# A two-block fp32 transformer kernel: output steps spread over the last attention heads, second weight slots waited for by pieces, one tile centred ahead of the roots, sixteen idle products, one gate copy released sooner

## The reference

```
block 1: mod = silu(c) @ ada_w + ada_b; h = rmsnorm(x)*(1+scale)+shift
         q,k,v,gates = h @ w_in; 8 sliding-window heads and 8 causal heads, d = 64
         x += gate1 * ((sig(ga)*(ya @ w_branch_a) + sig(gb)*(yb @ w_branch_b)) @ w_out)
         x += gate2 * (relu(h2 @ w_mlp_in)**2 @ w_mlp_out); x = rmsnorm(x)
block 2: short convolution mixer, layer_norm, SwiGLU (2816), layer_norm,
         forgetting attention (16 causal heads, logits + F[t] - F[s]) @ w_o, layer_norm,
         SwiGLU, layer_norm
```

## Time and profile before

| | us |
|---|---|
| median of 3 runs | 1969.68 (1968.35 to 1969.92) |
| the profiled execution, its own time | 1967.05 |
| its span, first to last instruction | 1965.3 |
| PE busy | 1906.1 (97%) |
| DVE busy | 1180.5 (60%) |
| ACT busy | 779.4 (40%) |
| POOL busy | 343.6 (17%) |
| mean granted TensorE clock | 0.992 |

### The profile page before, as it was taken

The page is one execution under the profiler, slowest core; times in us unless marked ns, Lnnn a source line. Parts: engine busy times, 40 slices in busy tenths (PEclk is TensorE's granted clock), DMA queues, the critical chain, the costliest instruction groups (busy, mean ns, idle before and its releaser), DMA issues.

```text
span 1965.3 us, 22312 instructions
## 1 busy us (share of the span) xinstructions
PE 1906.1 (97%) x8952; PEld 1577.2 (80%) x8952; DVE 1180.5 (60%) x1853; ACT 779.4 (40%) x1180; POOL 343.6 (17%) x307
## 2 busy tenths in 40 slices
PE   4999999999999999999999999999999999999997
PEld 3788888878888887888788888877898778888886
DVE  6687665576676745665655644476777754433446
ACT  4677622352223235222422222256677442222223
POOL 4323111021111112002300000036533130000003
PEclk9999999999999999999999999999999999999998
DMA  9522366266566434432545432313211223223221
GB/s 333 150 84 70 134 223 237 88 226 221 217 209 219 150 107 158 164 127 86 213 173 192 173 127 86 108 65 129 70 44 65 88 85 100 93 90 103 95 99 43
DMA packets 126232, 267.54 MB, mean 136 GB/s; under 512 B 4576, under 2 KB 33264, under 8 KB 126129
## 3 DMA queue, kind: packets, MB, share of 16 engines
q1 hardware_dynamic: 121168, 248.59, 37.0%
q0 software_dynamic: 4960, 17.53, 2.5%
HBM read 261.84 MB, written 8.45 MB: 138 GB/s over the span
## 4 chain that ended last, share of the span: by engine, by line
PE 70%; DVE 3%; ACT 2%; POOL 2%; issue 1%; DVEq 0%; POOLq 0%; ACTq 0%
PE ps L624 22%; PE ps L626 22%; PE ps L625 22%; PE ps L784 1%; PE ps L773 0%; ACT t L1212 0%; PE ps L762 0%; ACT t L1216 0%; POOL t L2316 0%; PE ps L801 0%; PE ps L802 0%; PE ps L800 0%; DVE t L1628 0%; DVE t L1613 0%; POOL t L2125 0%
## 5 line engine op out<-in xcount | busy, mean ns | idle before, releaser
L624 PE MATMUL ps<-t 128*128 128x512 f32 (+1 forms) x2504 | 966.7, 386 | 10.3 <-POOL t L2220 4.2
L626 PE MATMUL ps<-t 128*128 128x512 f32 (+1 forms) x2504 | 958.9, 383 | 0.0
L625 PE MATMUL ps<-t 128*128 128x512 f32 (+1 forms) x2504 | 955.0, 381 | 0.0
L1549 DVE TENSOR_TENSOR t<-t 128x2048 fp32r<-128x2048 f32 x133 | 305.4, 2296 | 440.4 <-ACT t L1163 440.2
L624 PEld LDWEIGHTS ps<-t 128*128 128x128 f32 x2504 | 470.7, 188 | 104.5 <-POOL t L2125 5.6
L626 PEld LDWEIGHTS ps<-t 128*128 128x128 f32 x2504 | 470.3, 188 | 96.4
L625 PEld LDWEIGHTS ps<-t 128*128 128x128 f32 x2504 | 470.5, 188 | 90.8 <-issue 1.0
L1163 ACT ACTIVATE t<-t 128x2048 fp32r<-128x2048 f32 x133 | 254.3, 1912 | 612.8 <-PE ps L626 605.3
L1613 DVE SCALAR_TENSOR_TENSOR t<-ps,t 128x512 f32<-128x512 f32 x184 | 131.7, 748 | 81.4 <-PE ps L626 78.0
L1561 DVE CUSTOM_DVE_ANT_0 t<-t 128x1024 f32<-128x1024 f32 x144 | 174.8, 1255 | 6.7 <-DMA t<-in_adakv_t 3.5
L2125 POOL TENSOR_TENSOR t<-t 128x512 fp32r<-128x512 f32 x88 | 115.5, 1332 | 196.8 <-ACT t L1170 196.2
(11 more groups left out here) (171 smaller groups left out, 1526.1 us busy)
## 6 DMA issues: line engine op xcount, KB each, us to landing
t<-in_ada SPq DMA_DIRECT2D x48, 1024.0 KB, 5.9
t<-in_gate SPq DMA_DIRECT2D x22, 1024.0 KB, 5.1
t<-in_up SPq DMA_DIRECT2D x22, 1024.0 KB, 5.1
t<-in_down SPq DMA_DIRECT2D x22, 1024.0 KB, 5.0
t<-in_w_in SPq DMA_DIRECT2D x17, 1024.0 KB, 5.7
t<-in_w_mlp_in SPq DMA_DIRECT2D x16, 1024.0 KB, 5.3
t<-in_w_mlp_out SPq DMA_DIRECT2D x16, 1024.0 KB, 5.0
t<-in_ada_t POOLq DMA_DIRECT2D x13, 1024.0 KB, 6.0
```

The source lines that it names most:

```text
L624: pe.matmul(o, wh, xh, start=first, stop=False)
L625: pe.matmul(o, wh, xl, start=False, stop=False)
L626: return pe.matmul(o, wl, xh, start=False, stop=last)
L1549: dve.tensor_tensor(WL[:, n % NW, :], raw[:, n % NRAW, :], WH[:, n % NW, :].bitcast(F), ALU.subtract).then_inc(w_lo_d.sem, w_lo_d.up("slot ...
```

## The change

It does five things. (1) The "o" job gets the units of kt 5 and 6, and the quotas of block 2 become 8 for heads 0 to 7, 7 for heads 8 to 11 and 2 for heads 12 to 15; after the last head only kt 7 is left of this slot. (2) `gemm_a` waits for the pieces of a pieced slot one by one, ahead of the tile that reads each. (3) In n4, n5 and n6 DVE centres one tile ahead of the wait for `rs`, and in the loop the next tile only. (4) Ahead of the third pair PE runs sixteen products of 256 columns. (5) ACT's copy of the gates waits for the first of the two writes of `AF`.

```diff
@@ job_units @@
             for kt in range(5):
                 yield ("unit", job, i, kt)
+        for kt in (5, 6):
+            for i in range(2):
+                yield ("unit", job, i, kt)
         return
-STEPS2 = attention_steps(["causal"] * 16, JOBS2, [8] * 12 + [3] * 4, AT_FOX + 3)
+STEPS2 = attention_steps(["causal"] * 16, JOBS2, [8] * 8 + [7] * 4 + [2] * 4, AT_FOX + 3)
@@ gemm_a @@
-                    slot_lo(on, n)
+                    pieced = n in PIECED
+                    if not pieced:
+                        slot_lo(on, n)
...
                         xh, xl, ready = src(kt)
+                        if pieced:
+                            on.wait_ge(w_lo_p, "slot", n, kt % 4)
@@ program_pe @@
-            for n, us in ((0, (0, 1)), (0, (2, 3)), (1, (0, 1, 2, 3)), (0, (4, 5)), (1, (4,)), (0, (6, 7)), (1, (5, 6, 7))):
+            for n, us in ((0, (0, 1)), (0, (2, 3)), (1, (0, 1, 2, 3)), (None, ()), (0, (4, 5)), (1, (4,)), (0, (6, 7)), (1, (5, 6, 7))):
+                if n is None:
+                    for _ in range(16):
+                        pe.matmul(psum[3][:, 0:256], ident, cst[:, 0:256], start=True, stop=True)
...
-                o_tile(AT_O, k, (5, 6, 7), 6 + k)
+                o_tile(AT_O, k, (7,), 6 + k)
@@ program_act @@
-            on.wait_ge(d_fox, "sum rows")
+            on.wait_ge(d_fox, "sum rows", 0)
@@ normed, program_dve @@
                 if layer:
-                    for k in range(3):
-                        centre(k)
+                    centre(0)
...
-                    if layer and k + 3 < KT:
-                        centre(k + 3)
+                    if layer and k + 1 < KT:
+                        centre(k + 1)
```

## The result

The changed kernel takes 1977.37 us (median of 4 runs, 1975.59 to 1978.97) beside 1969.01 for the kernel before (4 runs, 1966.61 to 1969.92): 8.36 us more, ratio 1.0041 with a 95% interval of 1.0028 to 1.0053. The forecast was 1972.7, in a range from 1968.5 to 1976.0. All medians are of executions in the fast state, which leaves out a single one of 7349 us, of the kernel before with one tile centred ahead.

What follows compares the result with a forecast made beforehand. PE, busy 97% of the span, was taken as the bound. Terms 6.9 - 0.75 - 0.55 - 0.2 - 0.6 - 1.8 + 0 = +3.0 took the profiled 1967.05 to 1970.05; plus 2.63 to the median: 1972.7 us, range 1968.5 to 1976.0.

Steps and rivals of the forecast that it cites:

- The products: Ahead of the third pair, sixteen idle products fill no wait and raise no clock, so cost their length: +6.9 us.
- the rival that hides them: At the third pair, the products cost nothing because a later PE wait takes the 6.9 back: 1965.8 us, chance 8%.
- Centring and pieces: One tile centred ahead gives n4 -0.75 us; pieces waited for singly give n4 -0.55, n3 -0.2, n6 -0.6.
- n5: Three centrings done by the roots' end, as in n6: 0.05 us at most, left out; no wait for pieces either.
- The units: Last heads: moved units fill 3.25 us of PE's idle time, a new wait ahead of kt 7 costs 1.45: -1.8.
- The first rival: Last heads: units lengthen the DVE and ACT chain and fill nothing, +1.45 for -1.8, time 1976.0 us, chance 14%.
- The gate copy: First gated head: ACT's copy comes sooner but isn't in the chain to PE's first score: 0, bound -0.3 us.
- The clock rival: Moved waits shift PE's half-clock stretches elsewhere, 1.8 to 3 us either way: 1970 or 1975.5 us, chance 12%.
- The sign: Whole kernel, beyond 0.2%: slower 0.30, faster 0.08, same 0.62.

Runs made afterwards that it cites:

- the fourth kernel: Changed kernel without the sixteen idle products and with three tiles centred ahead, keeping pieces, heads and gate copy: 1968.98 us beside 1970.25 before, ratio 0.9991.
- the kernel with three units: the fourth kernel plus three units of the next output slot ahead of the first kt 7: 1966.40 us beside 1969.39 before, ratio 0.9988.

## Why the prediction was wrong

**The products: right.** +6.9 was forecast from six records; the runs give 6.3 to 7.3, the timelines 6.7 to 6.9. They neither fill a wait nor hold a clock, and the rival that hides them is out.

**Centring and pieces: the step that failed.** They were to give -2.1 together (n4 -1.3, n3 -0.2, n6 -0.6) and gave +2.3 (n4 +0.64, n3 -0.05, n6 +1.73); that is 4.4 of the 5.4 us by which the sum was short (+8.36 for +3.0). The sentence is "The two added centrings take 0.3 to 0.6 of that". I had the time at which DVE ends tile 7's low half, 950.23, and the time at which PE wants it, and I moved only PE's. DVE was taken to have slack at the end because it has gaps there; they are used up by the two operations of 0.6 each, and then two more low halves fall behind POOL's operations. In the changed kernel the last low half is ready at 962.49. Moved back by the 10.8 that the kernel is late there, that is 951.7: 1.5 later than before, where at most 0.6 was allowed, while PE comes 1.9 sooner. And I looked at tile 7 alone; tiles 5 and 6 wait too, and with three tiles centred ahead the wait that is left (0.4) is tile 6's. The piece-wise wait by itself is worth about what was said, when three tiles are centred ahead: -0.70 for -0.55 in n4, -0.8 to -1.0 for -0.6 in n6, but -0.05 for -0.2 in n3. So is the first multiplication, 0.74 sooner for 0.75. The lock was weighed in the prediction for the centring only, whose length it doesn't touch (672 to 686 ns); what it does is to stretch the low halves that the centrings push on to POOL's operations.

**n5: a term put at nothing.** "n5 is alike" was read from a trace in which n5's roots ran at half clock, as those of n6 did, so that the three centrings were done in time. At full clock PE waits 0.79 there (the second trace of before), and the changed kernel is 0.66 faster. This goes the other way than the miss, and leaves some 0.7 of the medians' difference in no place.

**The units: right in mechanism, half in size.** -1.8 forecast, -0.85 measured. The new wait is 1.5 for 1.45. In heads 13 and 14 the idle time fell by 1.1 each and not by 1.38, in head 12 it grew from 0.20 to 0.37, and head 15's 0.29, which was to be filled, is 0.34. And "Heads 8 to 11 give up one unit each and wait for nothing" failed in head 9, a wait of 0.43 and a step of 0.6, which the kernel with the quotas of before doesn't have. The first rival isn't the reason: from one head's first value product to the next the time went from 6.18 to 6.20 and from 5.71 to 5.76 us, where DVE and ACT set the pace.

**The gate copy: right**, 0.0 within 0.1% in a run by itself.

**The clock rival** was right as a fact, that the stretches differ between the two traces, and wrong in its cause: they differ as much between two executions of the unchanged kernel, and the sum without them, 7.7, is inside the interval of the medians' difference. So they belong in the width of a trace and not among the effects of a change. But they decide what a change is worth: one tile ahead gains in n5 only at full clock, and its cost in n6 is 2.8 at half clock and 1.3 at full.

**The sign.** The chance for slower was 0.30, the bounds of n4 and n6 didn't reach below zero, and so the range ended at 1976.0. Had the bound on the other side been "the centrings cost all they take of DVE, 1.2 us, and one more stretched low half, 0.65", n4's term could have come out at +0.7 and n6's at +0.95, 2.8 above what was taken, and the range, with its upper end moved by as much to 1978.8, would have held 1977.4.

**What stays open.** The clean steps of the fourth kernel sum to -2.6 and those of the kernel with three units to -4.3; the runs say -1.3 and -3.0 by the medians. The first lies in its interval (0 to -3.5), the second just outside (-0.6 to -3.9), and both are 1.3 short. One trace of each can't tell whether stretches of low clock are more frequent in these kernels.

## What to carry to other kernels

An operation that is moved off one critical spot lands on another: follow the moved engine to the end of the stage, tile by tile, with the consumer's new and earlier time of need, and count its gaps as slack only after the added operations are in them. A term that is read where the clock is at 0.50 holds for that clock only: look for an execution that has 1.00 there. Where a wait shrinks, look at who is second, and give its arrival both its new delay and the other side's new demand. A unit of independent work is worth most where it covers a wait; moving it into one idle stretch uncovers another, which three units from the next tile covered at no cost (2.5 us in place of 0.85).

## What the runs showed of the hardware

The granted clock falls to 0.50 for short stretches, most of them at places that are the same in several traces when counted by the work done (38, 45, 140, 393, 1304, 1389 and 1583 us of before), but which of them an execution takes varies. One costs 0.9 to 1.6 us where PE has work (147, 400 and 1397 us of the changed kernel). Their ends apart, the two traces of the unchanged kernel have three and six of them, and two of the three (38 and 1304 us) are twice as long as the others. That this makes most of the scatter of its runs, 1965 to 1973 us, isn't shown, since only profiled executions show their clock by stage.

DVE's low halves and POOL's two-input operations can fall in step: once one low half was stretched from 0.68 to 1.34, the two cycles had the same length, 2.46 us, and the next two met as well. In n4, ahead of the last multiplication, one low half is stretched with three tiles centred ahead, two with two and three with one.
